# A two-layer hybrid trunk: end of the RWKV mixer by channel and token tile, shared expert's second half moved into the expert loop, norm rows loaded at routing

## The chip, the cores and the metric

The kernel runs on one core of a Trainium2 chip. The metric is the device time in microseconds (us) of one execution. Engine names: TensorE (PE; its weight loads are shown apart as PEld), VectorE (DVE), ScalarE (ACT), GpSimd (POOL) and SyncE (SP), whose queue issues most DMAs. All arithmetic is float32.

## The reference, cut to what matters

```python
def layer_norm(x, g, b):                     # over the 1024 channels of a token
    mu = mean(x); var = mean((x - mu) ** 2)
    return (x - mu) * rsqrt(var + LN_EPS) * g + b

# end of rwkv7_time_mix, y is (L, 16 heads, 64)
m = mean(y, -1); var = mean((y - m) ** 2, -1)
y = ((y - m) * rsqrt(var + GN_EPS)).reshape(B, L, D) * lnx_g + lnx_b
bonus = (sum(rh * kh * r_k, -1) * vh).reshape(B, L, D)
return ((y + bonus) * g) @ w_o

def moe_ffn(x2d, ...):                       # sigmoid scores, 8 of 64 experts a token, gates
    y = swiglu(x2d[tok], w_gate[e], w_up[e], w_down[e]) * gate      # each expert
    return swiglu(x2d, sh_gate, sh_up, sh_down) + routed_sum        # shared + routed

for i in range(2):                           # layer 0 mixes by RWKV-7, layer 1 by attention
    h = layer_norm(ALPHA * h + mix(h), ln_mix_g[i], ln_mix_b[i])
    h = layer_norm(ALPHA * h + moe_ffn(h), ln_ffn_g[i], ln_ffn_b[i])
```

There are 272 tokens (16 meta tokens, 256 of the sequence), 1024 channels, experts of width 256. Near the start of the RWKV mixer the 64-channel heads of k are also normalised: squares are summed a head, the root's reciprocal is spread over the head's channels and multiplied in.

## The kernel before, in words

Tokens lie in three tiles: 0 and 1 of 128 tokens, 2 of 16. Channels lie in eight groups c of 128 (two heads each). Each engine has its own program, written out in order; they wait for each other on counting semaphores. `rp`, `ra`, `rv` count the steps of TensorE, ScalarE and VectorE in the RWKV layer. A PSUM bank is reused eight steps later, once its reader is done (`r_evac`).

**Constants (GpSimd, L1203 to L1253).** Masks are made by memsets and `affine_select`s (`select`, recorded as L1220), among them `headrow` (L1248, L1249), which spreads a head's number over its channels. At the same time VectorE makes the shifted differences `xx` (L2158) and the first mixes (L2148); TensorE's key projection (L1382) waits for all eight of mix 2.

**Head sums and back.** `head_sums` (L1410) sums over the 64 channels of each head: eight matmuls of 272 tokens into 16 partitions. `to_channels` (L1418) goes back: eight matmuls with 16 rows of weights. Between them ScalarE takes a root and VectorE a reciprocal on 16x272. This is done for k (steps `n2s`, `n2`, multiplied in at L2198) and at the end for the variance (`vars`, `var`).

**End of the RWKV layer.** After the last state step: means (L1611), their subtraction (VectorE L2330), squares (ScalarE L1988), head sums, root, reciprocal (L2333), `to_channels`, three VectorE passes over the eight channel groups (L2335, L2339, L2343), then `out_projection` by quarters of the output columns: for each quarter tile 0 and tile 1, 128x256 a matmul (L1625), and at the end the 16 tokens of tile 2 (L1631). VectorE adds `ALPHA*h` a quarter at a time (L2351). When all is there, `ln` runs its steps over all three tiles at once (L2363 to L2381). `rv.end()` is the end of that.

**Attention's end (layer 1)** does its output projection (L1838) and norm tile by tile (`norm_tile`, L2606 to L2630).

**Routing.** From `rv.end()` (layer 0) or `av.end()` (layer 1) on: GpSimd clears and builds tables, TensorE turns h into `mhT` (channels by tokens) and multiplies by the router (L1653), VectorE picks groups and experts and computes for each expert which tokens it takes; GpSimd then gathers the 64 token rows of an expert by an indirect DMA (L805). In the pauses TensorE computes the shared expert (`mm_shared`, L984): first half of its width (`sg0`, `su0`) while VectorE routes, `sg1` just before the loop, `su1` in the turns of experts 0 and 1.

**Expert loop.** 64 turns. A turn of TensorE (`pe_expert`): gate and up (L768, 32 matmuls), turn the next expert's rows (L756), pick the slots of the one three ahead (L749), turn this expert's result (L775), down of the expert before (L786). Weights (3 MB an expert) go to four sets of three slots; SyncE issues gate and up of expert e+4 when expert e's gate and up are done, and down of e+4 when e's down is done (L829). The shared down matrix (1 MB) is issued after expert 3's weights, into `lnrow`, which later holds the rows g and b of the layer norm. Those (`load_ln`, L1256, L1257) are therefore loaded only after the shared down matmuls (L1680), by GpSimd.

**Layer end.** SyncE reads the routed results back (L1186, 8 MB); TensorE adds four of each token's eight rows (L1694), VectorE the other four (L2515), and both tiles are normalised after tile 2 (L2493 to L2503), which waits for `lnrow`.

## Time and profile before

| | us |
|---|---|
| runs | 1762.17 (1759.88, 1762.17, 1764.41) |
| profiled execution, its own time | 1763.27 |
| its span | 1761.4 |
| mean granted TensorE clock | 0.958 |
| TensorE busy | 1524.0 (87%) |
| VectorE busy | 643.3 (37%) |
| ScalarE busy | 339.4 (19%) |
| GpSimd busy | 318.8 (18%) |
| DMA | 508.02 MB, mean 288 GB/s |

A busy share is an average over stages with different limits. The span has these stages: RWKV to 438 us, routing to 466, experts of layer 0 to 982, its end to 1035, attention to 1162, routing to 1191, experts of layer 1 to 1706, its end to 1758. Granted clock 1.00 is TensorE's upper level of 2.4 GHz, 0.50 its lower of 1.2 GHz.

### The profile page before, as it was taken

The page shows a single profiled execution, that of the slowest core. Times are in us where ns is not written, and L with a number is a line of the kernel's source. Part 1 is how long each engine was busy: PE and PEld are TensorE (multiplying, and loading weights), DVE is VectorE, ACT ScalarE, POOL GpSimd, SP SyncE. Part 2 cuts the span into 40 slices and gives each one's busy share as a digit, 9 for nine tenths or more (in the row PEclk, how much of TensorE's full clock was granted, in tenths as well). Part 3 has the DMA queues.
Part 4 walks back from the last instruction along what each step waited for, and adds up shares of the span by engine and source line. Part 5 has one row for each costly group of instructions (what it writes and reads, how often), then busy time and mean ns, then how long its engine had stood idle before and what let it go on. Part 6 is the DMA issues. An engine that isn't in the chain of part 4 may idle for free.

```text
span 1761.4 us, 30841 instructions
## 1 busy us (share of the span) xinstructions
PE 1524.0 (87%) x11344; PEld 1027.4 (58%) x11344; DVE 643.3 (37%) x1632; ACT 339.4 (19%) x779; POOL 318.8 (18%) x394
## 2 busy tenths in 40 slices
PE   7999979877999888888888859989988888888884
PEld 5777979855765555555555327666555555555541
DVE  4443445444433332332332251463333323323325
ACT  2602333211111111111111103411111111111110
POOL 3012000000222222222222130022222222222210
PEclk9999989878999999999999969989999999999997
DMA  6520000023799999999999792179999999999975
GB/s 187 176 98 23 1 2 2 2 98 145 275 398 414 416 415 415 415 416 416 414 416 417 287 263 96 49 280 355 414 414 416 414 415 414 415 415 415 415 291 207
DMA packets 139852, 508.02 MB, mean 288 GB/s; under 512 B 29274, under 2 KB 58274, under 8 KB 104189
## 3 DMA queue, kind: packets, MB, share of 16 engines
q1 hardware_dynamic: 103600, 458.58, 65.3%
q0 software_dynamic: 22288, 41.89, 6.5%
q10 hardware_dynamic: 13884, 6.44, 1.4%
q8 instruction: 55, 0.90, 0.2%
q14 instruction: 25, 0.20, 0.0%
HBM read 501.38 MB, written 36.90 MB: 306 GB/s over the span
## 4 chain that ended last, share of the span: by engine, by line
PE 48%; DMA 38%; DVE 8%; issue 2%; SPq 2%; ACT 1%; POOL 1%; DVEq 0%; POOLq 0%; ACTq 0%
DMA arena<-in_moe_w_up 36%; PE ps L768 10%; PE ps L786 5%; PE ps L1382 5%; PE ps L1548 4%; PE ps L749 2%; PE ps L1625 2%; PE ps L1736 2%; PE ps L756 2%; PE ps L1838 2%; SPq L829 1%; DMA lnrow<-in_ln_ffn_b 1%; PE ps L1680 1%; DVE arena L2515 1%; PE ps L775 1%
## 5 line engine op out<-in xcount | busy, mean ns | idle before, releaser
L768 PE MATMUL ps<-arena 128*64 128x256 f32 x2048 | 234.7, 381 | 61.7 <-DMA arena<-in_moe_w_up 61.7
L768 PE MATMUL ps<-ring,arena 128*64 128x256 f32 x2048 | 234.7, 381 | 57.1 <-DMA ring<-in_moe_w_up 42.2
L761 DVE COPY arena<-ps 128x512 f32<-128x512 f32 x128 | 88.5, 691 | 508.8 <-PE ps L756 508.8
L768 PEld LDWEIGHTS ps<-arena 128*64 128x64 f32 x2048 | 165.3, 137 | 155.7 <-issue 112.6
L768 PEld LDWEIGHTS ps<-ring,arena 128*64 128x64 f32 x2048 | 155.2, 137 | 160.2 <-issue 84.0
L805 POOL DMA_INDIRECT arena<-hrows,arena x128 | 129.4, 1011 | 585.9 <-DVE arena L801 577.9
L810 POOL DMA_INDIRECT routed<-arena x128 | 117.7, 920 | 242.4 <-DVE arena L927 178.0
L927 DVE TENSOR_SCALAR arena<-ps,arena 64x512 f32<-64x512 f32 x128 | 95.1, 743 | 162.3 <-PE ps L786 162.3
L881 ACT COPY arena<-ps 128x256 f32<-128x256 f32 x128 | 47.6, 372 | 506.0 <-PE ps L768 506.0
L891 ACT ACTIVATE arena<-ps,arena 64x512 f32<-64x512 f32 x128 | 87.5, 683 | 206.1 <-PE ps L786 206.1
L786 PE MATMUL ps<-ring,arena 128*64 128x512 f32 x512 | 124.0, 605 | 0.0
L786 PE MATMUL ps<-arena 128*64 128x512 f32 x512 | 123.5, 604 | 0.0
L749 PEld LDWEIGHTS ps<-arena 128*128 128x128 f32 (+1 forms) x768 | 106.1, 190 | 6.0 <-DVE arena L793 2.4
L749 PE MATMUL ps<-arena 128*128 (+2 forms) x768 | 105.8, 242 | 3.1 <-DVE arena L793 2.1
L756 PE MATMUL ps<-ident,arena 128*128 128x128 f32 x512 | 83.9, 286 | 0.4 <-DMA arena<-hrows,arena 0.4
L756 PEld LDWEIGHTS ps<-ident,arena 128*128 128x128 f32 x512 | 53.7, 140 | 49.4 <-issue 48.5
L793 DVE SCALAR_TENSOR_TENSOR arena<-arena 128x384 f32<-128x384 f32 x128 | 69.3, 542 | 0.1
L885 ACT ACTIVATE arena<-ps 128x128 f32<-128x128 f32 x128 | 35.5, 277 | 152.4 <-PE ps L775 152.4
L1382 PE MATMUL ps<-arena,ring 128*128 128x272 f32 x256 | 61.8, 405 | 2.0 <-DVE arena L2198 1.5
L786 PEld LDWEIGHTS ps<-arena 128*64 128x64 f32 x512 | 31.2, 136 | 48.1 <-issue 48.1
L786 PEld LDWEIGHTS ps<-ring,arena 128*64 128x64 f32 x512 | 31.1, 136 | 47.2 <-issue 47.2
L1382 PEld LDWEIGHTS ps<-arena,ring 128*128 128x128 f32 x256 | 50.2, 197 | 13.6 <-DVE arena L2198 1.9
(383 smaller groups left out, 1825.9 us busy)
## 6 DMA issues: line engine op xcount, KB each, us to landing
ring<-in_moe_w_gate SPq DMA_DIRECT2D x64, 1024.0 KB
ring<-in_moe_w_up SPq DMA_DIRECT2D x64, 1024.0 KB
ring<-in_moe_w_down SPq DMA_DIRECT2D x64, 1024.0 KB
arena<-in_moe_w_gate SPq DMA_DIRECT2D x64, 1024.0 KB, 22.2
arena<-in_moe_w_up SPq DMA_DIRECT2D x64, 1024.0 KB
arena<-in_moe_w_down SPq DMA_DIRECT2D x64, 1024.0 KB
arena<-routed SPq DMA_DIRECT2D x16, 1024.0 KB, 14.6
ring<-in_attn_w_qkv SPq DMA_DIRECT2D x6, 1024.0 KB
```

Source lines behind the costliest of these rows:

```text
L749: mm = nc.tensor.matmul(dst[:, 0:3], hot[0:n, t, :], vals[0:n, t, :], start=(t == 0), stop=(t == NT - 1))
L756: mm = nc.tensor.transpose(dst[:, P * j:P * j + P], rows[:, P * j:P * j + P], ident[:, :])
L761: return nc.vector.tensor_copy(xgT.rearrange("p (r j) m -> p j r m", r=2), ps[:, bU, :].rearrange("p (j r m) -> p j r m", j=4, r=2))
L768: mm = nc.tensor.matmul(dst[SLOTS * j:SLOTS * j + SLOTS, 0:FF], xgT[:, k, :], slot_of(s + j)[:, FF * k:FF * k + FF], start=(k == 0), stop= ...
L786: mm = nc.tensor.matmul(dst[SLOTS * half:SLOTS * half + SLOTS, :], hid[:, j, :], slot_of(s)[:, D * j + 512 * half:D * j + 512 * half + 512 ...
L793: return nc.vector.scalar_tensor_tensor(out=hot, in0=iota_s[:, order, :].unsqueeze(1).to_broadcast([P, NT, 2 * SLOTS]), scalar=float(first ...
L805: return nc.gpsimd.indirect_dma_start(out=dst, out_offset=None, in_=hrows_d[l], in_offset=bass.IndirectOffsetOnAxis(ap=index, axis=0), bou ...
L810: return nc.gpsimd.indirect_dma_start(out=routed[l], out_offset=bass.IndirectOffsetOnAxis(ap=index, axis=0), in_=src, in_offset=None, boun ...
L891: nc.scalar.activation(ysc[q[1] % 4][:, 512:1024], ps[SLOTS:P, bY[q[1] % 2], :], ACT.Copy, scale=gate_s[q[1] % 8][SLOTS:P]).then_inc(L.y_a, 1)
L927: nc.vector.tensor_scalar(ysc[q[1] % 4][:, 0:512], ps[0:SLOTS, bY[q[1] % 2], :], gate_s[q[1] % 8][0:SLOTS], None, ALU.mult).then_inc(L.y_v, 1)
L1382: m = mm_(b[:, 0:T], slot3(s)[:, k, P * (c % 2):P * (c % 2) + P], xm[MIXBUF[mix]][:, k, :], start=(k == 0), stop=(k == KC - 1))
L1548: return lambda g, i, hd, b: mm_(b[0:n, P * i:P * i + n], lhs[g % 2][0:n, i, 0:n], rhs[g % 2][0:n, i, 0:n], start=True, stop=True)
```

## The change

1. `headcol` is 32 wide and `headrow` and `headnorm` hold their 16 rows four times, at partitions 0, 32, 64, 96, for four quarters of 68 tokens. `head_sums` makes four matmuls of 68 tokens for each of the old ones, into four column strips; `to_channels` four with 32 rows of weights, into four banks; VectorE reads the four banks in one instruction (`spread`). Root and reciprocal work on 128x68. `headrow` takes eight `affine_select`s on 32 rows instead of two on 16.
2. End of the RWKV layer: the table for the root is loaded before the squares; VectorE finishes the first four channel groups one after another, then the other four; the output projection takes tile 0 channel by channel for both halves of 512 columns as soon as a group is there, then the 16 tokens, then tile 1; residual and norm are `normalise`, tile by tile in the order 0, 2, 1, shared with attention. Routing's turns and PSUM banks of layer 0 follow that order.
3. `sg1` goes to the turns of experts 0 and 1, `su1` to those of experts 2 and 3; their readers move along.
4. The shared down matrix goes over `mhT`, whose last reader is `su1`; ScalarE issues its load in the turn of expert 4.
5. `lnrow` is then free: GpSimd loads the rows of `ln_ffn` right after the mixer's end, before its other clearing.

```diff
@@ constants (GpSimd)
-            select(headrow[:, :], None, ALU.is_ge, 0, -HD, [[1, D]])
-            select(headrow[:, :], None, ALU.is_ge, HD - 1, HD, [[-1, D]])
+            for j in range(4):
+                rows = headrow[32 * j:32 * j + 32, :]
+                select(rows, None, ALU.is_ge, 0, -HD, [[1, D]])
+                select(rows, None, ALU.is_ge, HD - 1, HD, [[-1, D]])
@@ head_sums, to_channels (TensorE)
-                    m = mm_(b[0:HEADS, 0:T], headcol[:, first:first + HEADS], src(c), start=(c == 0),
-                            stop=(c == C8 - 1))
-                m.then_inc(*rp.step(name))
+                    for j in range(4):
+                        m = mm_(b[32 * j:32 * j + 32, 0:QUARTER], headcol[:, first:first + 32],
+                                src(c)[:, QUARTER * j:QUARTER * j + QUARTER], start=(c == 0), stop=(c == C8 - 1),
+                                tile_position=(0, 32 * j))
...
+                for first in (0, 4):
+                    banks = [R(name, first + j) for j in range(4)]
+                    for c in range(4):
+                        for j, b in enumerate(banks):
+                            m = mm_(b[:, QUARTER * c:QUARTER * c + QUARTER],
+                                    headrow[32 * j:32 * j + 32, P * (first + c):P * (first + c) + P],
+                                    headnorm[32 * j:32 * j + 32, :], start=True, stop=True, tile_position=(32 * j, 0))
@@ r_evac: who frees the bank
-            if nm == "n2":
-                return rv.at("kk", u)
+            if nm == "n2":
+                return rv.at("kk", u | 3)
@@ output projection (TensorE)
+            both = [(R("o0", half), out_weights(half)) for half in range(2)]
+            for c in range(C8):
+                pe.wait_ge(*rv.at(f"yo{c}"))
+                for half, (b, w) in enumerate(both):
+                    m = mm_(b, yT[:, c, 0:P], w[:, :, 256 * c:256 * c + 256], start=(c == 0), stop=(c == C8 - 1))
...
+            for half in range(2):
+                b, w = R(f"o1_{half}"), out_weights(half)
+                for c in range(C8):
+                    m = mm_(b, yT[:, c, P:2 * P], w[:, :, 256 * c:256 * c + 256], start=(c == 0), stop=(c == C8 - 1))
+                m.then_inc(*rp.step(f"o1_{half}"))
@@ VectorE
+            for first in (0, 4):
+                for c in range(first, first + 4):
+                    V.tensor_tensor(quarters(yT[:, c, :]), quarters(yT[:, c, :]), spread("var", c), ALU.mult)\
+                        .then_inc(*rv.step(f"yn{c}"))
+                for c in range(first, first + 4):
...
+            for t in (0, 2, 1):
...
+                normalise(rv, ra, facc[0:n, t, :], t, add)
@@ pe_experts
-            pe.wait_ge(*moe_act[l].at("sg0"))
-            mm_shared(pe, l, "sg1", range(0, KC // 2))
             pe_pick(pe, L, (0, 2))
-            mm_shared(pe, l, "sg1", range(KC // 2, KC))
             pe_turn_x(pe, L, l, (0, 0))
...
-                if early(e, 0) or early(e, 1):
-                    mm_shared(pe, l, "su1", range(KC // 2 * e[1], KC // 2 * e[1] + KC // 2))
+                if isinstance(e[0], int) and e[1] < 4:
+                    mm_shared(pe, l, ("sg1", "su1")[e[1] // 2], range(KC // 2 * (e[1] % 2), KC // 2 * (e[1] % 2) + KC // 2))
@@ act_experts
+                if early(e, 4):
+                    act.wait_ge(*moe_pe[l].at("su1"))
+                    act.dma_start(shared_w[2], I["shared_w_down"][l].rearrange("(p j) n -> p (j n)", j=2))\
+                        .then_inc(shared_loaded[2], 16)
@@ GpSimd
                 nc.gpsimd.memset(score_T, 1.0).then_inc(score_cleared, 1)
+                load_ln(I["ln_ffn_g"][l], I["ln_ffn_b"][l])
...
                 pool_experts(pool, main, l)
-                pool.wait_ge(*moe_pe[l].end())
-                load_ln(I["ln_ffn_g"][l], I["ln_ffn_b"][l])
```

GpSimd's constants before (L1220 is the select, `headrow` the table that is replicated):

```order
L1220 AFFINE_SELECT notfirst<-notfirst 128x16
L1246 MEMSET headcol 64x1
L1247 MEMSET headcol 64x1
L1220 AFFINE_SELECT headrow<-headrow 16x1024 x2
L1220 AFFINE_SELECT small<-small 128x16 x2
```

And now (L1232 is the select):

```order
L1232 AFFINE_SELECT notfirst<-notfirst 128x16
L1258 MEMSET headcol 64x1
L1259 MEMSET headcol 64x1
L1232 AFFINE_SELECT headrow<-headrow 32x1024 x8
L1232 AFFINE_SELECT small<-small 128x16 x2
```

Two selects of 1024 elements became eight; all else keeps its place.

TensorE from the last state step to routing before: means (L1611), head sums (L1410), back to channels (L1418), output projection (L1625, 16 tokens L1631), turns of h (L1646):

```order
L1611 MATMUL ps<-arena,headones 128x272 x8
L1410 MATMUL ps<-arena,headcol 16x272 x8
L1418 MATMUL ps<-headnorm,headrow 128x272 x8
L1625 MATMUL ps<-ring,arena 128x256 x64
L1631 MATMUL ps<-ring,arena 16x256 x32
L1646 MATMUL ps<-ident,h 128x128 x16
L1646 MATMUL ps<-ident,h 128x16 x8
```

And now:

```order
L1632 MATMUL ps<-arena,headones 128x272 x8
L1424 MATMUL ps<-arena,headcol 32x68 x32
L1436 MATMUL ps<-headnorm,headrow 128x68 x32
L1647 MATMUL ps<-ring,arena 128x512 x16
L1653 MATMUL ps<-ring,arena 16x256 x32
L1659 MATMUL ps<-ring,arena 128x512 x16
L1671 MATMUL ps<-ident,h 128x128 x8
L1671 MATMUL ps<-ident,h 128x16 x8
L1671 MATMUL ps<-ident,h 128x128 x8
```

The 16 tokens stand between the two large tiles, and tile 1 is turned last.

TensorE at the start of the expert loop before (L749 picks, L984 the shared expert, L756 turn of rows, L768 gate and up):

```order
L749 MATMUL ps<-arena 128x3 x6
L984 MATMUL ps<-arena 128x272 x4
L749 MATMUL ps<-arena 128x3 x3
L984 MATMUL ps<-arena 128x272 x4
L756 MATMUL ps<-ident,arena 128x128 x4
L768 MATMUL ps<-ring,arena 64x256 x16
```

And now (L755, L762, L774, L781 and L985 are L749, L756, L768, L775 and L984 of before):

```order
L755 MATMUL ps<-arena 128x3 x9
L762 MATMUL ps<-ident,arena 128x128 x4
L774 MATMUL ps<-ring,arena 64x256 x16
L762 MATMUL ps<-ident,arena 128x128 x4
L755 MATMUL ps<-arena 128x3 x3
L781 MATMUL ps<-ident,arena 128x128 x2
L985 MATMUL ps<-arena 128x272 x4
```

Nothing stands any more between the picks and the turn of expert 0's gathered rows; turns 0 to 3 each hold four matmuls of the shared expert, where turns 0 and 1 did.

## Rows read from the trace of the kernel before

**Rows 1.** Page, part 4: the chain that ended last, by line.

```profile
DMA arena<-in_moe_w_up 36%; PE ps L768 10%; PE ps L786 5%; PE ps L1382 5%; PE ps L1548 4%; PE ps L749 2%; PE ps L1625 2%; PE ps L1736 2%; PE ps L756 2%; PE ps L1838 2%; SPq L829 1%; DMA lnrow<-in_ln_ffn_b 1%; PE ps L1680 1%; DVE arena L2515 1%; PE ps L775 1%
```

**Rows 2.** Chain of waits, end of layer 0's mixer: start, us, what.

```profile
363.21 5.71 PE ps L1611 x16
...
370.05 3.84 PE ps L1410 x16
...
374.42 1.85 DVE headnorm L2333
...
376.32 6.94 PE ps L1418 x16
...
389.89 29.96 PE ps L1625 x128
419.86 3.62 PE ps L1631 x64
...
434.28 3.68 DVE h L2381 x3
```

**Rows 3.** Chain of waits, end of layer 1's mixer.

```profile
1143.38 13.95 PE ps L1838 x32
...
1160.43 1.29 DVE h L2629
```

**Rows 4.** Timeline, small matmuls in row and column strips: start, us, engine, line.

```profile
166.66 4.74 PE L1537 MATMUL ps<-arena 64*128 64x128 f32 x80
...
355.18 1.15 PE L1469 MATMUL ps<-arena,ring 64*64 64x64 f32 x32
```

**Rows 5.** Timeline, end of layer 1; in brackets idle time and releaser.

```profile
1730.28 9.74 PE L1694 MATMUL ps<-arena,ident 128*128 128x512 f32 x16 [3.78 <-DMA arena<-routed]
...
1732.59 1.27 DVE L2493 BATCH_NORM_STATS2 small<-arena 16x6 f32<-16x512 f32 x2 [12.35 <-DMA lnrow<-in_ln_ffn_b]
...
1750.00 1.28 DVE L2524 TENSOR_TENSOR arena<-arena,ps 128x512 f32<-128x512 f32 x2
```

**Rows 6.** Timeline, VectorE and GpSimd while `headrow` is made, and TensorE's wait.

```profile
14.46 1.33 DVE L2148 SCALAR_TENSOR_TENSOR h<-arena,small 128x272 f32<-128x272 f32 x1
14.46 2.22 POOL L1220 TENSOR_SCALAR_AFFINE_SELECT headrow<-headrow 16x1024 f32<-16x1024 f32 x2
...
15.71 1.27 DVE L2158 TENSOR_TENSOR arena<-arena 128x272 f32<-128x272 f32 x1
...
17.43 0.44 DVE L2158 TENSOR_TENSOR arena<-arena 128x272 f32<-128x272 f32 x1
...
23.86 8.52 PE L1382 MATMUL ps<-arena,ring 128*128 128x272 f32 x36 [0.58 <-DVE arena L2148]
```

**Rows 7.** Timeline, VectorE's product and TensorE's wait before v.

```profile
104.98 2.86 DVE L2198 TENSOR_TENSOR arena<-arena,ps 128x272 f32<-128x272 f32 x8
105.52 31.77 PEld L1382 LDWEIGHTS ps<-arena,ring 128*128 128x128 f32 x128 [1.86 <-DVE arena L2198]
```

**Rows 8.** Timeline, GpSimd's first gather in layer 0.

```profile
457.30 1.18 POOL L805 DMA_INDIRECT arena<-hrows,arena  x1 [10.23 <-DVE arena L801]
```

**Rows 9.** Chain of waits, first gather and first gate and up in layer 1.

```profile
1182.57 6.81 DMA arena<-hrows,arena
...
1190.92 3.67 PE ps L768 x32
```

**Rows 10.** Stretch 1182.5 to 1185: busy of PE, PEld, DVE, ACT, POOL; clock; DMA share, GB/s.

```profile
1182.50:1185.00 2.50, 2.50 (x7) 1.95 (x7) 0.34 (x3) 0.00 (x0) 2.13 (x2) 0.52 1.05 428
```

**Rows 11.** Chain of waits, first turn of layer 0.

```profile
466.12 3.67 PE ps L768 x32
...
471.40 1.84 PE ps L984 x8
```

**Rows 12.** Timeline, SyncE's issues of down for experts 6 and 7.

```profile
496.40 0.38 SPq L829 DMA_DIRECT2D arena<-in_moe_w_down  x1
...
503.33 0.38 SPq L829 DMA_DIRECT2D arena<-in_moe_w_down  x1
```

More of the change, by code:

```diff
@@ L42 @@
 CHUNK = 32
+QUARTER = T // 4
 HALF = 16
@@ L66 @@
 TAIL = 3
-LN_STEPS = 8
 ARENA = 30956
@@ L1984, in _ @@
                         .then_inc(*ra.step(f"m_{t}", j))
+            A_(small[:, 250:251], eps[:, 0:1], ACT.Sqrt)
             for c in range(C8):
@@ new lines, in normalise @@
+            def normalise(sv, sa, acc, t, add):
+                n = TILES[t][1]
+                for half in range(2):
+                    if t < NT - 1 or not half:
+                        add(half, slice(512 * half, 512 * half + 512) if t < NT - 1 else slice(0, D))\
+                            .then_inc(*sv.step(f"res{half}_{t}"))
+                        dve.wait_ge(*sv.at(f"res{half}_{t}"))
+                    V.bn_stats(stat[0:n, t, 6 * half:6 * half + 6], acc[:, 512 * half:512 * half + 512])\
+                        .then_inc(*sv.step(f"st{half}_{t}"))
+                dve.wait_ge(*sv.at(f"st1_{t}"))
+                V.bn_aggr(mv[0:n, t, :], stat[0:n, t, :]).then_inc(*sv.step(f"mv_{t}"))
+                dve.wait_ge(*sv.at(f"mv_{t}"))
+                V.scalar_tensor_tensor(out=acc, in0=acc, scalar=mv[0:n, t, 0:1], in1=lnrow[0:n, 0, :],
+                                       op0=ALU.subtract, op1=ALU.mult).then_inc(*sv.step(f"sub_{t}"))
+                dve.wait_ge(*sa.at(f"std{t}"))
+                V.reciprocal(rstd[0:n, t:t + 1], std[0:n, t:t + 1]).then_inc(*sv.step(f"rec_{t}"))
+                dve.wait_ge(*sv.at(f"rec_{t}"))
+                V.scalar_tensor_tensor(out=h[0:n, t, :], in0=acc, scalar=rstd[0:n, t:t + 1], in1=lnrow[0:n, 1, :],
+                                       op0=ALU.mult, op1=ALU.add).then_inc(*sv.step(f"out_{t}"))
@@ new lines, in _, with add @@
+            dve.wait_ge(h_loaded, 64)
+            dve.wait_ge(ln_loaded, 32)
+            for t in (0, 2, 1):
+                n = TILES[t][1]
+                def add(half, cs):
+                    if t == NT - 1:
+                        dve.wait_ge(*ra.at("fw"))
+                        projected = few_o[0]
+                    else:
+                        projected = got("o0", half) if t == 0 else got(f"o1_{half}")
+                    return V.scalar_tensor_tensor(out=facc[0:n, t, cs], in0=h[0:n, t, cs], scalar=ALPHA, in1=projected,
+                                                  op0=ALU.mult, op1=ALU.add)
+                normalise(rv, ra, facc[0:n, t, :], t, add)
@@ L2390, in moe @@
+            dve.wait_ge(*rv.end())
             def moe(l):
```

245 lines of the change are left out of this document (93 added, 152 removed).

## The prediction, made before the changed kernel ran

> **What bounds the kernel now.** I read first the page's chain by line: the largest entry is the weights' DMA, 36% [rows 1]. The middle of each expert loop is a DMA stream. TensorE starts with four experts loaded and then waits for weights, so what counts of the loop is when its stream starts, where it stalls and what it carries. It starts when expert 0's gate and up are done. Second, the chain in order of time around the change: at the end of layer 0's mixer it is serial, one engine at a time [rows 2], where layer 1's mixer ends with projection and norm overlapped [rows 3]. Third, the timeline of the layer ends: VectorE sits idle for 12.35 us for `lnrow`, and as long in layer 0's [rows 5]. Fourth, the timeline near the start, where GpSimd's constants are made [rows 6]. All sums are made against the profiled execution's 1763.27 us (span 1761.4), which lies 1.1 above the median.
>
> **A. More selects while VectorE mixes: +3.9.** The two `headrow` selects take 2.22 us, 1.11 each. The two VectorE operations beside them take 1.33 and 1.27, the same operation later 0.44 [rows 6]. So one of them passes a select. Six more selects hold six more operations for 1.11 instead of 0.45: 6 x 0.66 = 3.9. Behind VectorE stands TensorE's key projection, which waited 0.58 for it already, so nothing hides the shift. Bounds: 0, if only these two collided by chance, and 6.7, if the six selects only add up. The row shows operations with two SBUF inputs slowed to a select's length. The Trainium skill (SBUF — State Buffer, who interferes with whom) says why: such an operation and a GpSimd operation that reads SBUF share a port pair that is locked for a whole instruction. By this rule every new select holds one operation, the 3.9 above; without it the two rows could be chance, and the term 0.
>
> **B. The same sums for k: -0.5.** Here the order of TensorE is full, so shorter matmuls count. Eight matmuls, 16 records since a float32 matmul makes two, in 3.84 us (the same line, [rows 2]) become 32 of 68 tokens, 64 records. Matmuls in strips went at 1.15/32 = 0.036 each in 64x64, at 4.74/80 = 0.059 in 64x128 [rows 4]. At 0.036 the sum takes 2.3, a gain of 1.5 (between 0 and 1.5). But v's first bank is now freed by the fourth product of VectorE instead of the first: three more at 2.86/8 = 0.36, and TensorE stood there waiting for it [rows 7]: +1.1. `to_channels` of k is hidden behind that wait. Together -0.4 to -0.5, bounds -1.5 and +1.1.
>
> **C. End of the RWKV layer: -24.8.** Means end at 363.21 + 5.71 = 368.9 and stay. Squares follow the means one by one now and then too; the head sums, 2.3 instead of 3.84, run to 371.2 (they were held by squares before). The root took the 0.5 between 373.89, the head sums' end, and 374.42, and takes 0.4; the reciprocal has 68 columns for 272: 1.85 x 68/272 = 0.5, to 372.1. `to_channels` of the first four groups is 32 records at 0.059 = 1.9, to 374.0 (at the lower clock twice that; 6.94 before). VectorE: four products and the first group's other two passes, six operations at 0.4 (0.36 in [rows 7]), 2.4, to 376.4. The projection took 29.96 and 3.62 for the 16 tokens. With 512 columns layer 1's costs 13.95 a tile [rows 3], so 27.9 + 3.6 = 31.5; I add 1.0 for a start at the lower clock (0 to 2.1, since 29.96 - 27.9 = 2.1 is what it cost before), to 408.9. VectorE needs some 0.8 a group and TensorE 13.95/8 = 1.7, so from here TensorE sets the pace. Behind the last matmul stands one tile's norm, in layer 1 from 1143.38 + 13.95 = 1157.3 to 1160.43 + 1.29 = 1161.7, 4.4. Mixer's end at 413.3 where it was 434.28 + 3.68 = 438.0 [rows 2]. The norms of tiles 0 and 2 lie under tile 1's matmuls. Range -20 to -27.
>
> **D. From the mixer's end to expert 0.** Layer 0: first gather at 457.30, 19.3 after the mixer's end [rows 8]; layer 1: 1182.57, 20.9 after [rows 3, 9]. Layer 0 now ends as layer 1 does, with a large tile last, and weights still streaming: I take 20.9, +1.5. GpSimd's two more issues (its clearing sets the pace in layer 0 within a us) go into that; bounds 0 and 2.7. Then, in layer 1, the gather lands after 6.81 and gate and up end at 1190.92 + 3.67 = 1194.6, 12.0 after the gather's issue; in layer 0 466.12 + 3.67 = 469.8, 12.5 after [rows 11]. `sg1` stood in that gap. Its removal from there gives nothing in layer 1, since the gather lands last, and at most 0.5 in layer 0. What it hid comes out: after the picks TensorE is idle until the gather lands, and the clock falls anyway in that stretch, mean 0.52 of the upper level [rows 10], that is at 1.2 GHz; `sg1` brought it back. Now the turn and gate and up start at the lower level: 3.67 of full-speed work costs up to 3.7 more, I take +2.0 (0 to 4). So layer 0: +1.5 and 12.0 + 2.0 - 12.5 = +1.5; layer 1: +2.0. Sum D +5.0.
>
> **E. In the loop: +9.2.** `su1`'s half costs 1.84 in this record of a turn [rows 11]; with its gaps I take 2.0. Turns 0 and 1 had them before and have `sg1` now: 0. Turns 2 and 3 are new. SyncE's issues of down follow TensorE 6.93 apart (503.33 - 496.40), [rows 12]; now 8.9. The 3 MB they belong to need 3.15/0.428 = 7.4 at least at the rate of [rows 10], with gathers and scatters more. The stream was just covered and now runs dry twice. Bounds 0 and 2 x 2.0 = 4.0, I take 2.1. The shared down matrix used to come in the pause before the loop, at no cost; now it lies in the stream: 1.05 MB/0.428 = 2.5. Its place in the pause is taken by `lnrow`, the same size. Per layer 4.6, twice 9.2.
>
> **F. Layer ends: -24.7.** VectorE's 12.35 go in either layer if nothing else is late next. Next are the routed rows: TensorE got tile 1's first piece at 1730.28 - and waited for it - with `lnrow`'s 1 MB in the same queues [rows 5]. VectorE took tile 1's sums from PSUM at 1750.0; 12.35 sooner it wants them at 1737.7. The matmuls ended at 1730.28 + 9.74 = 1740.0, in part at the lower clock, and come at least 2.5 sooner without `lnrow` (1 MB, worked out under E). So they are just in time, and the gain is full; bounds -20 and -24.7.
>
> Sum: +3.9 - 0.5 - 24.8 + 5.0 + 9.2 - 24.7 = -31.9; 1763.27 - 31.9 = 1731.4, and from the median 1730.3. I say 1731.
>
> **Rivals.**
> 1. GpSimd's selects do not hold VectorE (A is 0): 1727. For it: only two operations show it. Against: both are as long as a select, to 0.2 us.
> 2. The clock stays up at the projection and at the loop starts: -1.0 and twice -2.0, 1726. For it: head sums and spreads give TensorE something to do. Against: [rows 10].
> 3. The layer ends give back part, since VectorE meets the routed rows late (F -18 instead of -24.7), or the loop's stalls go to their upper bound (+4): some +10, 1741. For it: TensorE's wait in [rows 5].
> 4. No gain: the projection now interleaves with VectorE's groups, and the array stays at the lower clock all through it: 31.5 more, 1762. Against: before, the same stretch was back at speed within 2.1 us of loss.
> 5. Slower: with nothing left between picks and expert 0, the array stays at 1.2 GHz in the first turns, where small matmuls alternate with waits. A turn of 6.93 + 2.0 = 8.9 becomes some 16, and the stream, which needs some 8, stalls 7 to 8 a turn. Four turns in two layers cost 60: 1791. It decides from five such turns in both layers on (5 x 7.5 = 37 against 31.9 gained and 5.3 of margin). For it: [rows 10]. Against: before, gate and up in the first turn took 3.67 [rows 11], right after such a stretch, with only `sg1` between.
>
> **How the numbers follow.** Forecast 0.45 (own range 1726 to 1737), rival 1 0.14, rival 2 0.13, rival 3 0.20, rival 4 0.03, rival 5 0.05. The range of 8 in 10 takes in rivals 1 to 3 and half of C's bounds: 1720 to 1744. What this kernel's runs tell from no change is about 0.3%, 5.3 us. Faster: all but rivals 4 and 5, 0.92; same 0.03; slower 0.05.
>
> **What would show it.** In the profile after: eight selects from 14.5 to 23.4, VectorE's operations beside them 1.1 to 1.3 long, the key projection at 27.8 (A). Means to mixer's end 50 us instead of 75 (C); one root's table load ahead of the squares. First gather 20.9 after the mixer's end in both layers; first gate and up 5 to 6 us long at a clock of 0.5 to 0.8 (D). DMA share below 1 after the fourth turn, and down's issues 9 us apart (E). No wait of VectorE for `lnrow`, the norm of tile 2 right after its few rows, TensorE's waits for `routed` as before (F). Wrong: if VectorE waits for routed rows for more than 3 us, if the expert loop, from its first gate and up to its last, is over 8 us longer than before (4.6 expected), or if the key projection starts before 25.

## The result: 27.5 us less, and where they are

The changed kernel took 1733.53 us (median of 4 runs, 1731.85 to 1735.73), the kernel before beside it 1761.03: ratio 0.9844, 95% interval 0.9818 to 0.9870. Six more runs of it in another series (e9) had a median of 1742.20 against 1761.33, 0.9892 (0.9868 to 0.9915). So the gain is real, and its size is known to some 8 us only. The forecast was 1731, in 1720 to 1744. The traces are sharper than the medians: cut at the events of the program, most stages of the two profiled runs of this kernel agree to a few tenths of a us, and what they differ by lies in the RWKV layer ahead of its end (last section). The profiled run after took 1735.73 (span 1734.0), 27.5 less than the one before.

| stage (us, profiled runs) | before | after | difference | forecast |
|---|---|---|---|---|
| start to end of key projection | 53.5 | 57.7 | +4.3 | A +3.9 |
| from there to r's projection | 17.2 | 14.5 | -2.7 | B, both rows: -0.5 |
| r's to v's projection | 34.9 | 36.0 | +1.05 | |
| v's projection to the means' end | 263.4 | 261.7 | -1.6 | none |
| means' end to mixer's end, layer 0 | 69.0 | 44.7 | -24.4 | C -24.8 |
| mixer's end to first gather, layers 0 and 1 | 19.4, 20.9 | 22.2, 23.4 | +2.9, +2.6 | D +1.5, 0 |
| first gather to end of first gate and up | 12.5, 12.0 | 14.4, 14.9 | +1.9, +2.9 | D +1.5, +2.0 |
| first to last gate and up | 508.0, 507.1 | 511.9, 511.4 | +4.0, +4.3 | E +4.6, +4.6 |
| last gate and up to the layer's end | 56.9, 59.7 | 45.2, 48.6 | -11.7, -11.1 | F -12.35, -12.35 |
| attention | 127.1 | 127.4 | +0.3 | none |

An event is the end of an instruction, or the start of the gather's issue on GpSimd; layer 1's end is the last instruction of all, 3.1 us of storing behind its last norm.

The page's chain by line of the changed kernel, against [rows 1]: the entry of `lnrow` is gone, and the wait for the routed rows has come up. The projection is not gone: L1647 and L1659 took 16.45 and 13.95 us (C below), together as long as L1625 took. What went is the time in front of it and behind it.

```profile
DMA arena<-in_moe_w_up 36%; PE ps L774 11%; PE ps L1395 5%; PE ps L792 5%; PE ps L1569 5%; PE ps L755 2%; DMA arena<-routed 2%; SPq L835 2%; PE ps L762 2%; PE ps L1761 2%; PE ps L1863 2%; PE ps L1719 1%; PE ps L985 1%; PE ps L781 1%; PE ps L1647 1%
```

**A, against [rows 6].** Timeline of the changed kernel, VectorE, GpSimd and TensorE (start, us, engine, line; in brackets idle time and releaser), then busy times by stretch (the last three numbers are the granted clock, the DMA share and GB/s).

```profile
14.81 0.50 DVE L2178 SCALAR_TENSOR_TENSOR h<-arena,small 128x272 f32<-128x272 f32 x1
15.23 1.28 DVE L2188 TENSOR_TENSOR arena<-arena 128x272 f32<-128x272 f32 x1
16.54 1.16 DVE L2178 SCALAR_TENSOR_TENSOR h<-arena,small 128x272 f32<-128x272 f32 x1
...
15.17 9.53 POOL L1232 TENSOR_SCALAR_AFFINE_SELECT headrow<-headrow 32x1024 f32<-32x1024 f32 x8
...
26.70 31.03 PE L1395 MATMUL ps<-arena,ring 128*128 128x272 f32 x128 [5.38 <-DVE arena L2178]
```

```profile
26.00:30.00 4.00, 3.30 (x8) 2.56 (x9) 4.00 (x11) 0.00 (x0) 1.30 (x2) 0.57 0.51 186
30.00:40.00 10.00, 10.00 (x46) 8.28 (x45) 3.25 (x8) 2.87 (x8) 0.00 (x0) 1.00 0.09 35
```

As forecast, operations of VectorE beside the eight selects are as long as a select: seven with two inputs in SBUF take 1.16 to 1.28; one, at 0.49, came through between two selects. What was not: after 5.38 us of waiting the granted clock is 0.57 in 26 to 30 us, the lower level for most of that stretch, and the projection takes 31.03 us for 29.60.

The two traces also differ ahead of all selects, by when the tokens have landed. Timeline of TensorE, first the changed kernel, then the kernel before:

```profile
7.72 6.76 PE L1383 MATMUL ps<-ident,arena 128*128 128x128 f32 x24 [7.72 <-DMA arena<-in_x]
```

```profile
9.53 6.76 PE L1370 MATMUL ps<-ident,arena 128*128 128x128 f32 x24 [9.53 <-DMA arena<-in_x]
```

VectorE's first difference starts at 9.24 for 10.97 before. From there to the key projection's start it is 17.46 us for 12.90, so the selects cost 4.6, and the earlier landing hides 1.7 of it.

**C, against [rows 2].** Chain of waits of the changed kernel, from the means to the mixer's end.

```profile
364.45 5.45 PE ps L1632 x16
369.90 0.97 PE ps L1424 x56
372.35 1.25 PE ps L1436 x32
373.69 1.48 DVE arena L2367 x4
376.20 16.45 PE ps L1647 x32
392.65 3.58 PE ps L1653 x64
396.23 13.95 PE ps L1659 x32
...
413.29 1.30 DVE h L2394
```

TensorE's two waits in that stretch, timeline, and the clock behind them:

```profile
372.35 2.02 PE L1436 MATMUL ps<-headnorm,headrow 32*128 32x68 f32 x64 [1.13 <-DVE headnorm L2363]
376.20 16.45 PE L1647 MATMUL ps<-ring,arena 128*128 128x512 f32 x32 [1.83 <-DVE arena L2374]
```

```profile
376.00:380.00 4.00, 3.80 (x5) 1.77 (x6) 3.90 (x11) 0.00 (x0) 0.00 (x0) 0.50 0.00 0
384.00:388.00 4.00, 4.00 (x11) 1.81 (x10) 0.00 (x0) 0.00 (x0) 0.00 (x0) 1.00 0.00 0
```

The projection starts 6.3 us after the means where I had 7.5. Tile 0 takes 16.45 for 13.95: the lower clock costs 2.5, not 1.0.

**D, against [rows 8 to 11].** Timeline of VectorE and GpSimd after the mixer's end (414.57) in layer 0, then the chain of waits from the gather on in layer 0.

```profile
415.22 3.50 DVE L2433 COPY arena<-h 128x1024 f32<-128x1024 f32 x1
418.65 0.67 DVE L2426 COPY arena<-ps 128x512 f32<-128x512 f32 x1
...
414.89 0.56 POOL L1270 DMA_DIRECT2D lnrow<-in_ln_ffn_g  x1
415.45 0.54 POOL L1271 DMA_DIRECT2D lnrow<-in_ln_ffn_b  x1
415.97 1.94 POOL L1304 MEMSET arena<- 128x512 f32 x4
417.82 0.93 POOL L1305 MEMSET arena<- 128x1 f32 x1
```

```profile
436.79 6.81 DMA arena<-hrows,arena
443.64 1.13 PE ps L762 x4
444.79 0.70 DVE arena L767
445.54 5.60 PE ps L774 x32
```

The copy of `h` for the row store (L2433) takes 3.50 us here and 3.58 in layer 1; before it took 1.49 and 1.12:

```profile
438.59 1.49 DVE L2410 COPY arena<-h 128x1024 f32<-128x1024 f32 x1
```

In both layers it ends within 0.03 us of the last of the memsets shown (418.72 and 418.75 here). Behind it on VectorE stands the last piece of the transposed h, and behind that the router. Then gate and up run cold as forecast: 5.60 here, 6.31 in layer 1.

**E, against [rows 12].** Timeline of SyncE's issues of down in the third and fourth turn, then busy times by stretch.

```profile
470.82 0.38 SPq L835 DMA_DIRECT2D ring<-in_moe_w_down  x1
...
479.94 0.38 SPq L835 DMA_DIRECT2D arena<-in_moe_w_down  x1
```

```profile
470.00:480.00 10.00, 10.00 (x65) 5.76 (x62) 2.54 (x8) 1.79 (x5) 2.75 (x3) 1.00 0.97 378
520.00:560.00 40.00, 37.20 (x276) 23.21 (x276) 13.51 (x39) 7.12 (x17) 9.68 (x10) 1.00 1.02 414
```

The turns with `sg1` and `su1` are 9.1 us apart, and the stream moves 378 GB/s in them where it moves 414 later.

**F, against [rows 5].** Timeline of layer 1's end.

```profile
1713.05 10.19 PE L1719 MATMUL ps<-arena,ident 128*128 128x512 f32 x16 [2.78 <-DMA arena<-routed]
...
1703.97 1.27 DVE L2516 BATCH_NORM_STATS2 small<-arena 16x6 f32<-16x512 f32 x2
...
1722.48 1.48 DVE L2547 TENSOR_TENSOR arena<-arena,ps 128x512 f32<-128x512 f32 x2 [1.13 <-PE ps L1719]
```

The norm of the few rows no longer waits, and VectorE meets tile 1's sums 1.13 us too early.

### The profile page after: what moved, and what is told of

Its sections match the earlier page's. It is cut to its first block, busy times and chain, and to the rows that moved or that the text cites. A ratio compares the mean times of both kernels' runs of the same rounds, so it can differ in the third digit from the quotient of the medians.

```text
span 1734.0 us, 31109 instructions
## 1 busy us (share of the span) xinstructions
PE 1514.4 (87%) x11472; PEld 1009.8 (58%) x11472; DVE 650.7 (38%) x1629; ACT 340.5 (20%) x782; POOL 327.1 (19%) x400
## 4 chain that ended last, share of the span: by engine, by line
PE 48%; DMA 39%; DVE 7%; SPq 2%; issue 2%; ACT 1%; ACTq 0%; POOL 0%; POOLq 0%; DVEq 0%
DMA arena<-in_moe_w_up 36%; PE ps L774 11%; PE ps L1395 5%; PE ps L792 5%; PE ps L1569 5%; PE ps L755 2%; DMA arena<-routed 2%; SPq L835 2%; PE ps L762 2%; PE ps L1761 2%; PE ps L1863 2%; PE ps L1719 1%; PE ps L985 1%; PE ps L781 1%; PE ps L1647 1%
## 5 line engine op out<-in xcount | busy, mean ns | idle before, releaser
L774 PE MATMUL ps<-arena 128*64 128x256 f32 x2048 | 234.7, 381 | 62.5 <-DMA arena<-in_moe_w_up 62.5
L774 PE MATMUL ps<-ring,arena 128*64 128x256 f32 x2048 | 239.4, 387 | 55.8 <-DMA ring<-in_moe_w_up 40.8
L774 PEld LDWEIGHTS ps<-arena 128*64 128x64 f32 x2048 | 164.8, 137 | 156.2 <-issue 112.7
L774 PEld LDWEIGHTS ps<-ring,arena 128*64 128x64 f32 x2048 | 157.1, 139 | 161.3 <-issue 85.4
L755 PEld LDWEIGHTS ps<-arena 128*128 128x128 f32 (+1 forms) x768 | 106.5, 192 | 6.8 <-DVE arena L799 2.4
L755 PE MATMUL ps<-arena 128*128 (+2 forms) x768 | 106.7, 243 | 4.2 <-DVE arena L799 2.1
L762 PE MATMUL ps<-ident,arena 128*128 128x128 f32 x512 | 84.9, 289 | 8.7 <-DMA arena<-hrows,arena 8.7
L762 PEld LDWEIGHTS ps<-ident,arena 128*128 128x128 f32 x512 | 54.2, 142 | 57.4 <-issue 48.5
L799 DVE SCALAR_TENSOR_TENSOR arena<-arena 128x384 f32<-128x384 f32 x128 | 69.1, 541 | 0.1
L792 PEld LDWEIGHTS ps<-ring,arena 128*64 128x64 f32 x512 | 31.1, 136 | 47.3 <-issue 47.3
## 6 DMA issues: line engine op xcount, KB each, us to landing
ring<-in_attn_w_qkv SPq DMA_DIRECT2D x6, 1024.0 KB, 11.9
```

What stands on the lines that cost most here:

```text
L755: mm = nc.tensor.matmul(dst[:, 0:3], hot[0:n, t, :], vals[0:n, t, :], start=(t == 0), stop=(t == NT - 1))
L762: mm = nc.tensor.transpose(dst[:, P * j:P * j + P], rows[:, P * j:P * j + P], ident[:, :])
L774: mm = nc.tensor.matmul(dst[SLOTS * j:SLOTS * j + SLOTS, 0:FF], xgT[:, k, :], slot_of(s + j)[:, FF * k:FF * k + FF], start=(k == 0), stop= ...
L792: mm = nc.tensor.matmul(dst[SLOTS * half:SLOTS * half + SLOTS, :], hid[:, j, :], slot_of(s)[:, D * j + 512 * half:D * j + 512 * half + 512 ...
L799: return nc.vector.scalar_tensor_tensor(out=hot, in0=iota_s[:, order, :].unsqueeze(1).to_broadcast([P, NT, 2 * SLOTS]), scalar=float(first ...
```

## The experiments

Twelve runs in three series, each timed against the kernel before; e9 is the changed kernel again. The edits of e1 to e5 are small against the spread of the runs, so the stage in which each edit stands is the measure, and the medians are given beside it. Each cell with two numbers is layer 0 and layer 1. The first three columns are times from the start, the others lengths of stages.

| kernel | key proj. ends | r's starts | means end | mixer after means | gather after mixer | gate, up end after gather | loop | layer end |
|---|---|---|---|---|---|---|---|---|
| before | 53.5 | 70.6 | 368.9 | 69.0 | 19.4, 20.9 | 12.5, 12.0 | 508.0, 507.1 | 56.9, 59.7 |
| after | 57.7 | 72.2 | 369.9 | 44.7 | 22.2, 23.4 | 14.4, 14.9 | 511.9, 511.4 | 45.2, 48.6 |
| e9 | 59.0 | 76.8 | 378.8 | 44.7 | 22.3, 23.4 | 14.4, 15.1 | 511.7, 511.0 | 45.4, 47.4 |
| e1 | 59.6 | 77.4 | 372.8 | 44.8 | 21.2, 20.5 | 15.0, 14.4 | 511.8, 511.4 | 45.1, 47.3 |
| e2 | 58.3 | 72.8 | 373.8 | 44.8 | 21.2, 20.8 | 15.0, 14.5 | 511.6, 511.3 | 45.6, 47.3 |
| e3 | 59.2 | 77.0 | 375.2 | 44.9 | 22.4, 23.1 | 14.5, 11.8 | 510.5, 509.2 | 45.9, 47.4 |
| e4 | 50.8 | 65.3 | 366.2 | 44.7 | 22.2, 23.3 | 14.4, 14.9 | 511.9, 511.3 | 45.7, 47.4 |
| e5 | 58.9 | 76.7 | 375.4 | 44.7 | 22.2, 23.1 | 14.4, 14.9 | 509.9, 508.7 | 46.5, 47.3 |
| e6 | 58.8 | 78.3 | 381.9 | 44.6 | 21.1, 20.8 | 12.2, 11.9 | 508.4, 506.9 | 56.6, 59.5 |
| e7 | 51.3 | 65.7 | 360.1 | 44.6 | 21.1, 20.6 | 12.6, 14.6 | 508.1, 507.3 | 45.5, 47.4 |
| e8 | 50.5 | 65.0 | 359.2 | 42.4 | 20.6, 20.5 | 14.5, 14.6 | 507.9, 507.0 | 45.1, 47.4 |
| e10 | 52.7 | 73.2 | 365.9 | 69.1 | 24.2, 24.3 | 11.2, 14.8 | 512.3, 511.0 | 45.4, 47.4 |
| e11 | 52.9 | 70.7 | 372.7 | 42.4 | 21.2, 20.1 | 14.5, 11.8 | 508.1, 506.9 | 45.7, 47.4 |
| e12 | 50.4 | 64.9 | 362.0 | 42.4 | 19.7, 20.1 | 13.2, 14.6 | 508.5, 507.8 | 45.0, 47.3 |

**e1: GpSimd loads the norm rows behind its tables.**

```diff
-                load_ln(I["ln_ffn_g"][l], I["ln_ffn_b"][l])
...
                     .then_inc(route_consts, 1)
+                load_ln(I["ln_ffn_g"][l], I["ln_ffn_b"][l])
```

> The changed kernel, with GpSimd's two loads of the norm rows moved from in front of its memsets to behind its last table select. In the changed kernel VectorE's copy of h (128x1024) after the mixer took 3.50 and 3.58 us in layers 0 and 1 where it took 1.49 and 1.12 before, and the router's matmuls behind it start 4.9 us after the mixer's end instead of 2.8 and 2.7. Theory G: what holds VectorE is GpSimd making those two loads at the same time. Then the copy is back at 1.1 to 1.5 us, the router's matmuls at 2.7 us, the first gather at 19.3 to 20.9 us after the mixer's end (22.2 and 23.4 in the changed kernel), and the time is 1729 us (4.5 less than 1733.5). Rival O: the delay comes from the new order of tiles at the mixer's end. Then the copy stays at 3.5 us and the time at 1733 to 1734.

The copy is back, timeline of e1 in layer 1:

```profile
1139.90 1.11 DVE L2433 COPY arena<-h 128x1024 f32<-128x1024 f32 x1
```

The gather comes 1.0 and 2.9 us sooner; median 1732.11, ratio 0.9844 (0.9824 to 0.9863), no difference that the medians can show. Theory G holds. In layer 0 the gather stays 1.8 later than before: the router took 4.11 us, for 2.18 before, behind waits of 2.61 and 1.43 us of TensorE.

**e2: the same load at the same time, issued by ScalarE.**

```diff
+                    if t == H_ORDER[l][-1]:
+                        act.wait_ge(*prev_dve.end())
+                        act.dma_start(lnrow[:, 0, :], row(I["ln_ffn_g"][l])).then_inc(ffn_ln_loaded, 16)
+                        act.dma_start(lnrow[:, 1, :], row(I["ln_ffn_b"][l])).then_inc(ffn_ln_loaded, 16)
...
```

(GpSimd's call is taken out, and VectorE waits for the new semaphore.)

> The changed kernel, with the two loads of the norm rows issued by ScalarE instead of GpSimd, at the same place in time (right after the mixer's end). The same 1 MB moves at the same time, but GpSimd does not issue it. Theory G (GpSimd's issuing holds VectorE's copy of h): the copy is back at 1.1 to 1.5 us, and the first gather at 20 to 21.5 us after the mixer's end; 1729 to 1731 us. Rival M (the traffic of the load, or its place before the weights, holds the copy or the stores of h): the copy stays at 3.5 us and the time at 1733 to 1735.

```profile
1139.57 0.37 ACTq L2044 DMA_DIRECT2D lnrow<-in_ln_ffn_g  x1
1139.97 0.51 ACTq L2045 DMA_DIRECT2D lnrow<-in_ln_ffn_b  x1
1140.18 1.48 DVE L2437 COPY arena<-h 128x1024 f32<-128x1024 f32 x1
```

The loads are issued as early as in the changed kernel, and the copy behind them takes 1.48. So it is not the traffic but that GpSimd issues (median 1733.19, which shows no difference). The Trainium skill (SBUF — State Buffer, who interferes with whom) says that such a copy can want the port pair that VectorE shares with GpSimd, and that DMAs from hardware queues don't need it; 1.48 for 3.58 agrees. It also says that the pair is held for one instruction; in the changed kernel the copy began beside the first load and ended with the fifth memset behind the loads, so it was held over a row of instructions.

All traces bear this out. In the six in which GpSimd issues the loads right behind the mixer (after, e3, e4, e5, e9, e10) the copy takes 3.50 to 3.58 in both layers, and GpSimd's memsets of 128x512 some 0.54 each. In the eight others it takes 1.11 to 1.49, and one such memset beside it takes 1.3 to 1.5: there GpSimd waits. e10 has the old order of tiles in layer 0, so that order is not the cause. The one exception is layer 0 of e11: 2.45 beside the memsets, with no load issued. So the issues decide who waits, but the memsets can hold the copy too; what exactly lets GpSimd keep its turn is not shown.

**e3: sg1 back in the gap before the loop**, su1 in turns 0 and 1, with the waits that belong to them.

```diff
+            pe.wait_ge(*moe_act[l].at("sg0"))
+            mm_shared(pe, l, "sg1", range(0, KC // 2))
             pe_pick(pe, L, (0, 2))
+            mm_shared(pe, l, "sg1", range(KC // 2, KC))
             pe_turn_x(pe, L, l, (0, 0))
```

> The changed kernel, with the second half's gate (sg1) back between the picks before the expert loop and its up half (su1) back in turns 0 and 1. Theory D: in the changed kernel the first gate and up took 5.60 and 6.31 us at the lower clock instead of 3.67, and the loop from the first gate and up to the last was 4.0 and 4.3 us longer, 2.5 of it the shared down matrix. Then here the first gate and up are back at 3.7 us in both layers (1.9 and 2.6 gained) and the loop is 1 to 1.6 us shorter than in the changed kernel, in sum 6 to 8 us less: 1726 to 1728 us. Rival S: DMA sets the loop however the turns are filled, and gate and up start cold anyway; then at most 2 us less.

```profile
1173.30 3.67 PE L774 MATMUL ps<-ring,arena 128*64 128x256 f32 x32 [0.78 <-DVE arena L767]
```

Gate and up run at full speed in both layers, and the loop is 1.4 and 2.1 us shorter. The first gate and up end 3.1 sooner after the gather in layer 1, but not in layer 0: there `sg1` itself ran at the lower clock (4.00 and 3.90 a half) and pushed them back. The gain from the gather to the last gate and up is 1.3 and 5.2, in sum 6.5 of the 6 to 8. The profiled run (1735.29) doesn't show it, since its r's projection started 4.8 later than in the trace after and its mixer ended 5.5 later; nor does the median (1735.03), and whether the other runs lost the same is not shown.

**e4: the headrow selects where VectorE is idle**, with a wait of `to_channels` for them.

```diff
             pool.dma_start(biasd, brow).then_inc(bias_stored, 16)
+            pool.wait_ge(*rv.at("rn"))
+            for j in range(4):                      # the eight selects, unchanged
+                ...
+            pool.nop().then_inc(*consts.step("rows"))
```

> The changed kernel, with the eight headrow selects moved to where VectorE is idle (behind the reciprocal of k's norms, some 73 to 82 us), in front of their only reader. Theory A: the selects beside VectorE's mixes made the key projection start 2.84 us later (26.70 for 23.86) and run 1.43 longer (31.03 for 29.60), 4.3 in sum. Then here the key projection starts at 23.9 and takes 29.6, v's projection starts at about 104, and the time is 1729 to 1730 us (4.3 less). Rival: the selects slow VectorE by chance only, or what is gained is waited for again before v; then the time stays within 1.5 us of 1733.5.

```profile
15.46 0.43 DVE L2192 TENSOR_TENSOR arena<-arena 128x272 f32<-128x272 f32 x1
...
21.22 29.60 PE L1398 MATMUL ps<-arena,ring 128*128 128x272 f32 x128
...
65.96 8.75 POOL L1232 TENSOR_SCALAR_AFFINE_SELECT headrow<-headrow 32x1024 f32<-32x1024 f32 x8 [11.92 <-DVE headnorm L2220]
```

The key projection ends at 50.8: 6.9 us sooner than after, and 2.6 sooner than before. Of these 2.6, 1.2 are the two old selects, which had held VectorE as well (11.69 us from its first difference to the projection, for 12.90), and 1.4 are tokens that landed sooner. v's projection starts at 101.27 for 108.18, so nothing is waited for again up to there. From there to the means this trace takes 264.9 for 261.7, so 3.2 of the 6.9 don't reach the mixer; that stretch differs by up to 10 us between traces (last section). Median 1731.59, ratio 0.9838: a gain that the medians can't show.

**e5: the shared down matrix behind the last expert's weights**, by SyncE.

```diff
             over_experts(sp, lambda e: sp_expert(sp, L, l, e))
+            sp.wait_ge(*moe_pe[l].at("su1"))
+            sp.dma_start(shared_w[2], I["shared_w_down"][l].rearrange("(p j) n -> p (j n)", j=2))\
+                .then_inc(shared_loaded[2], 16)
...
```

(ScalarE's issue in turn 4 is taken out.)

> The changed kernel, with the shared down matrix (1 MB) issued by SyncE behind the last expert's weights instead of by ScalarE in turn 4. Theory L: in the stream it delays every expert behind it by 2.5 us per layer, while behind the last expert's down it lands before TensorE needs it (TensorE has 7.8 us of work from the landing of the last up on, and down and shared down need 5.0). Then from the first gate and up to the last is 509.4 us in layer 0 and 508.9 in layer 1 (511.9 and 511.4 in the changed kernel, 507.9 and 507.1 before) and the shared matmuls start as soon after the last gate and up as now; 5 us less in sum, 1728.5 us. Rival: the loop's extra time is from the turns with sg1 and su1, or the end waits for the matrix by as much; then 1733 us.

The loop is 2.0 and 2.7 us shorter; in layer 1 the shared matmuls start at 1692.92 right behind the last down. The median (1738.48) is above the changed kernel's; in its profiled run the 5 us are lost ahead of the means.

**e6: the RWKV part alone** and **e10: the expert part alone.** In e6 the edits of the expert part are undone; e10 is the kernel before with them.

> The changed kernel with only its part in the RWKV layer: the expert part (sg1 in the turns, down matrix over the transposed h, norm rows loaded early) is as before. By the terms as the changed kernel's trace gives them (start to the means +1.0, end of the mixer -24.4, first gather 1.9 later at most) the mixer of layer 0 ends at 413.6 to 418 us, VectorE waits 12.35 us for the norm rows at both layer ends, and the time is 1736 to 1740 us, 21 to 25 less than before's 1761. The expert part is then worth -3 to -6 us. Rival: the two parts are not additive, and the expert part is worth nothing or costs; then 1733 or less.

> The kernel before with only the change's expert part: sg1 and su1 in turns 0 to 3, down matrix over the transposed h, norm rows loaded right behind the mixer's end. Theory: the parts are additive, and the wait for the norm rows (2 x 11.4 gained) is mostly paid for by colder starts, longer turns, the matrix in the stream and VectorE's slower copy. From the mixer's end to the layer's end it took 596.7 and 599.7 us before and 593.7 and 598.4 in the changed kernel; expected here 594 and 598.4, and in sum 4 to 5 us less than before: about 1756. Rival: it is worth 10 us or more by itself (as the difference of 12 us between the medians of the run without this part and of the changed kernel says).

From the mixer's end to the layer's end: 596.7 and 599.7 before, 598.3 and 599.1 in e6, 593.1 and 597.5 in e10, 593.7 and 598.4 after (e9: 593.7 and 596.9). The expert part is worth 4 to 7 us by stages. By medians, e6 is 1746.11, above the 1736 to 1740 expected (ratio 0.9914, 0.9883 to 0.9945) and e10 1753.75 (0.9956, 0.9935 to 0.9977), so by itself it gives 7.6 of 1761.3, and the two parts together (0.9914 x 0.9956 = 0.9870) lie between the two results of the changed kernel. That fits two parts that add; the 12.6 us between the medians of e6 and after is not all the expert part, since the e6 profile alone lost 12.0 us before the means.

**e9: the changed kernel again.**

> The changed kernel once more, beside the next one. The runs of one kernel spread over 4 to 14 us so far, more than what most single edits move, while stages with no part in an edit repeat within a few tenths. Expected: 1731 to 1736 us; from the mixer's end to the end of layer 0, 593.7 us, and from layer 1's mixer's end on, 598.4 us, each within 1 us; the spread sits in the stretch from 57 us to the means.

The median, 1742.20, is above what I expected. Behind the mixer layer 0 is as expected (593.7); layer 1, 596.9, is 1.5 below, more than the 1 us allowed, with 1.2 of it in the layer's end. From the key projection's end to the means it takes 319.8 for 312.2: there the spread sits, as expected.

**e7: the edits of e1, e3, e4 and e5 together.**

> The changed kernel with four edits: norm rows loaded behind the tables, sg1 back before the loop with su1 in turns 0 and 1, shared down matrix behind the last expert's weights, headrow selects where VectorE is idle. If they add up as their stages have shown: selects -5.5, copy of h -1.0 and -2.9, sg1 -1.7 and -5.0, down matrix -5.0, in sum -21: 1712.5 us. If the weights' stream or the layer ends take part of it back: 1716 to 1724.

1714.70 us, ratio 0.9748 (0.9714 to 0.9782). By stages they add up: the key projection ends 6.5 sooner, and the stages behind the mixer give 6.4 and 8.5, in sum 21.4 where 21 was expected; the median is 18.8 below the changed kernel's. The loop is as short as before the change, and the layer ends keep their gain.

**e8: e7, and TensorE's waits at the RWKV layer's end filled** with matmuls whose result nobody reads.

```diff
+            def keep_warm(n):
+                for _ in range(n):
+                    mm_(spare_bank[0], ident[:, :], headrow[:, 0:512], start=True, stop=True)
...
                 for first in (0, 4):
+                    if name == "var" and first:
+                        keep_warm(2)
...
             head_sums("vars", lambda c: A[0][:, c, :], ra, "ysq")
+            spare_bank.append(psum_of(rp, "vars", 1))
+            keep_warm(1)
```

> The kernel of the four edits, with three matmuls whose result nobody uses (ident by 512 columns of headrow) in TensorE's waits at the RWKV layer's end: one between the head sums and the reciprocal, two between the two halves of to_channels. In the changed kernel TensorE's clock was 0.80 and then 0.50 in 372 to 380 us, after waits of 1.1 and 1.8 us, and the projection of tile 0 took 16.45 us instead of 13.95. Theory K: it is those waits that let the clock fall. Then the projection of tile 0 takes 14.0 to 14.8 us, and the mixer ends 1.7 to 2.5 us sooner after the means (44.7 in the changed kernel, so 42.2 to 43). Rival: so short a wait isn't what lets the clock fall, or the extra matmuls come out on the path; then the tile takes 16 us still, or the mixer's end is the same or up to 1.7 us later.

```profile
360.46 1.13 PE L1433 MATMUL ps<-headrow,ident 128*128 128x512 f32 x2
361.65 1.12 PE L1446 MATMUL ps<-headnorm,headrow 32*128 32x68 f32 x32
362.71 1.98 PE L1433 MATMUL ps<-headrow,ident 128*128 128x512 f32 x4
...
365.68 14.00 PE L1659 MATMUL ps<-ring,arena 128*128 128x512 f32 x32
```

```profile
366.00:370.00 4.00, 4.00 (x10) 1.72 (x9) 3.90 (x11) 0.00 (x0) 0.00 (x0) 1.00 0.00 0
```

Where the clock stood at 0.50, it stands at 1.00, and tile 0 takes 14.00. The mixer ends 2.3 sooner. Theory K holds; 1713.85, 0.9743.

**e11: e8, and three such matmuls in the wait for the last tile's norm. e12: e11, with only one half of sg1 in the gap.**

```diff
+                    if t == H_ORDER[l][-1]:
+                        for _ in range(3):
+                            mm_(ps[:, 6, :], ident[:, :], headrow[:, 0:512], start=True, stop=True)
                     pe.wait_ge(*h_ready(l, t))
```

> The kernel with the four edits and the busy gaps, and three more unused matmuls in TensorE's wait of 2.6 us for the last tile's norm, at both mixers' ends. By theory K the eight transposes behind it take 1.0 us instead of 2.0, and the router's matmuls 2.2 instead of 3.9; the first gather comes 1.5 to 2.2 us sooner after the mixer's end (20.6 and 20.5 without them), in sum 3 to 4 us less. Rival: behind the router stands GpSimd's table work, which now decides; then at most 1 us.

> The same kernel, with only one half of sg1 in the gap before the loop, its other half in turn 0 and su1's halves in turns 1 and 2. With both halves in the gap, at the lower clock, the first gate and up started 10.9 us after the first gather; the gather has landed after 6.8, and in the changed kernel they started 8.7 after it but ran 5.6 to 6.3 us. If one half keeps the clock up: start 8.7 after the gather and 3.7 long, 2.2 us sooner per layer, and one more turn of 2 us beside the weights' stream, of which 0.5 to 1 comes out: 2 to 3 us less in sum. Rival: the clock falls again while TensorE waits for the gather; then gate and up take 5 to 6 us and nothing is gained.

Layer 1 of e11, TensorE:

```profile
1131.85 1.16 PE L1686 MATMUL ps<-ident,h 128*128 128x128 f32 x8
1134.64 2.18 PE L1693 MATMUL ps<-arena,router 128*64 128x144 f32 x32 [1.64 <-DVE arena L2442]
```

Here the transposes and the router go at full speed, but the router waits for VectorE instead, and the gather comes 0.4 us sooner. In layer 0 it comes 0.6 later: there VectorE's copy of `h` took the 2.45 us told under e2, and the router behind it 3.50. e12 has the same three matmuls and no such copy; its router takes 2.18 in both layers and its gather comes 0.9 and 0.4 sooner than in e8. So the rival (at most 1 us, for 3 to 4) was near in its number, with VectorE's copies as the next wait, not GpSimd's tables. In layer 1 of e11 gate and up then end 2.8 sooner after the gather than in e8 (11.8 for 14.6), since the second half of `sg1` took 2.11 for 4.00. That the three matmuls did this is not shown: e3 has 11.8 without them. In e12 gate and up started 8.1 and 8.3 us after the gather and took 5.08 and 6.36: half of `sg1` doesn't keep the clock up, as its rival said. e11 is 1713.57, 0.9713 (0.9687 to 0.9740), e12 1714.35, 0.9753. e7, e8, e11 and e12 can't be told apart by these runs; all beat both kernels; e11 is 1.8% below the changed kernel of the same series by the two ratios, 1.6% by the two medians.

## Why the prediction held, step by step

**What bounds it**: right. What was gained or lost ahead of the loop's stream, in it and behind it adds up to the 27.4 us between the spans.

**A**: mechanism right (e4), size short: 4.3 in this trace, 4.9 to 6.1 in the six other traces with early selects, for 3.9. VectorE's delay itself was sized well: from its first difference to the key projection it is 17.3 to 17.5 in all seven, 4.4 to 4.6 more than before. What failed was to stop there: the wait of 4.3 to 5.4 us it gives TensorE costs 1.4 to 2.7 of clock on top. That 4.3 came so near to 3.9 is luck, since the tokens landed sooner than in the trace before and took 1.7 off (0.9 to 1.5 in the others).

**B**: the head sums took 1.15 where I took 2.3: 64 records at 0.018 each, half of the 0.036 that [rows 4] give in 64x64. The fourth product's +1.1 came as +1.05. So -1.6, just past the bound of -1.5. Where the clock fell in this stretch (last section) 3.3 are lost again. The head sums of k, timeline of the changed kernel:

```profile
67.27 1.15 PE L1424 MATMUL ps<-arena,headcol 128*32 128x68 f32 x64
```

**C**: -24.4 for -24.8 (the prediction's own end of 413.3 gives -24.7). The clock's part is 2.5 where I took 1.0 (past its bound of 2.1). Most of that miss was made up for in front of it: the head sums ended 1.4 after the means for 2.3, and VectorE could start on the first four groups after 1.25 of `to_channels` for 1.9. The number held by two errors that cancel, the overlap was right.

**D**: the term that was mis-sized, 10.2 for 5.0. Three quarters of the miss, 3.9 of 5.2, is a mechanism the prediction passed by: I put GpSimd's two issues into 1.5 us and asked what queues behind them on GpSimd, not what they hold on VectorE. e1 shows them at 1.0 and 2.9, and e2 at 1.0 and 2.6. The 1.5 I took for layer 0 is there without them: 1.8 in e1, nearly all of it the router's 4.11 for 2.18. The cold start is 1.9 and 2.9 for 1.5 and 2.0, shown by e3 in layer 1.

**E**: 8.3 for 9.2. e5 gives the matrix 4.7 of them (5.0 forecast), e3 the turns 3.6 (4.2).

**F**: -22.8 for -24.7, in its bounds. In every other trace with the rows loaded early layer 1's end took 47.3 to 47.4, the full 12.35 less than 59.7; the changed kernel's own trace, with 48.6, is the exception: TensorE's sums of tile 1 took 10.19 us there and 7.13 in e5. Layer 0's end never gave all of it: 45.0 to 46.5, where 44.5 would.

**Rivals**: 1 (selects don't hold VectorE) and 2 (clock stays up) are refuted by the rows above, 5 (slower) by the 9.1 us turns and the 4 us of loop. The error of the sum, 4.4 us (27.5 for 31.9), is D's 5.2, F's 1.9 and some 1.1 of A, C and attention, against E's 0.9, B's 1.1 and the 1.6 ahead of the means; so errors cancel in it too. Rivals 3 and 4 didn't come either: the layer ends kept 22.8 of 24.7, and the projection was back at full speed by 384 us. That 1731 lay 2.5 from the median says less than it seems: the same kernel gave 1742.2 in another series.

## What to carry to other kernels

Ask of each DMA that GpSimd issues what VectorE copies at that moment; from ScalarE's queue, or a few us later, the same load didn't hold that copy. A transfer that is needed only at the end of a stream belongs behind the stream; work that can fill a wait in front of the stream belongs into the wait, not into the stream. Where edits are worth less than the spread of the runs, cut the traces at events and compare stage by stage.
